# Two-block transformer on one core: gather, bias product and first expert weights reordered, neighbourhood scores computed two steps ahead, modulation groups regrouped

## The chip, the cores and the metric

The kernel runs on one core of one Trainium2 chip. The metric is the device time of one execution in microseconds (us), as the median of the runs. Engines by their names in the profile: PE is TensorE, DVE VectorE, ACT ScalarE, POOL GpSimd, SP SyncE, which here only starts transfers.

## What is computed

A batch of one with 256 tokens of width 1024 passes two blocks, all in fp32. The first block has a modulated mixer, a router that sends each token to 4 of 32 experts, and the experts. The second has two layers with modulated feed-forwards (SwiGLU, inner width 2816). Its layer 0 mixes by neighbourhood attention, which also looks at 256 context tokens, beside a multi-scale pool; its layer 1 by a short convolution. Cut to what the change touches:

```python
def moe_ffn(h, router_w, router_b, w1, b1, w2, b2):
    ...
    logits = (xt @ router_w + router_b).astype(jnp.float32)
    top_v, top_e = lax.top_k(logits, TOP_K)
    gate = jax.nn.softmax(top_v, axis=-1)
    ...
        hb = xb @ w1[e] + b1[e]
        ...
        return ((u + 1.0) * glu) @ w2[e] + b2[e]

def second_block(...):
    for i in range(DEPTH_2):
        m_l = adaln(c[:, None, :], mod_w[i], mod_b[i])         # 9 groups of 1024
        m_c = adaln(c_ctx[None, None, :], mod_w[i], mod_b[i])
        x = ffn_sublayer(x, m_l, norm_g[i, 0], ffn_w13[i, 0], ffn_w2[i, 0], 0)
        if ctx_here:
            ctx = ffn_sublayer(ctx, m_c, norm_g[i, 0], ffn_w13[i, 0], ffn_w2[i, 0], 0)
        xn = modulate(rms_norm_2(x, norm_g[i, 1]), m_l[:, :, 3], m_l[:, :, 4])
        if even:
            cn = modulate(rms_norm_2(ctx, norm_g[i, 1]), m_c[:, :, 3], m_c[:, :, 4])
            y_l, y_c = even_mixer(xn, cn, even_w_in[e], even_w_out[e], na_rpb[e], pool_w[e], pool_scale[e], ctx_out)
        ...
        x = x + m_l[:, :, 5] * y_l
        x = ffn_sublayer(x, m_l, norm_g[i, 2], ffn_w13[i, 1], ffn_w2[i, 1], 6)

def even_mixer(hl, hc, w_in, w_out, rpb, pool_w, pool_scale, ctx_out):
    q, k, v, u = jnp.split(hl @ w_in, [NA_WIDTH, 2 * NA_WIDTH, 3 * NA_WIDTH], axis=-1)
    k_c, v_c = jnp.split(hc @ w_in[:, NA_WIDTH:3 * NA_WIDTH], 2, axis=-1)
    att = neighbourhood_attention(split_heads(q), split_heads(k), split_heads(v), k_c, v_c, rpb)
    pool = multiscale_pool(u, pool_w, pool_scale)
    y_lat = jnp.concatenate([att, pool], axis=-1) @ w_out
```

## The kernel before

**Weights and ring.** All weights pass once through a ring in the on-chip memory. SP starts one transfer of 1 MB for each slot (128 partitions x 2048 numbers); in the experts and behind them the ring has eight places, and a transfer starts when the slot that held its place is released. The order of the slots in the stream is made ahead of the run by `make_plan` (class `Plan`), which also numbers the uses of PSUM.

**Products in parts.** From the experts on, an fp32 product is made of rounded parts: ScalarE copies a slot into one of four `w_high` buffers (L911 in the experts, L1005 later), VectorE subtracts that from the slot in place and gets `w_low` (L2228, L2364), and TensorE multiplies high by high, high by low and low by high (`split_gemm`, L1190; in the experts `w_high` and `w_low` by the gathered tokens `xg`, L1554). The activations' parts are `h_high` (ScalarE, `split_h`, L1018) and `h_low` (VectorE, `low_part`, L1871). Some products take fp32 straight from the ring, in one part (`gemm`, L1144).

**PSUM.** It is used in four places of two banks each, in strict rotation: use number u ("unit") takes place u mod 4, signals `psum_full` when TensorE has written it, and `psum_free` of its place when ScalarE or VectorE has read it.

**Order.** Nothing is scheduled by a tool. Each engine runs its own hand-written sequence, and semaphores keep the sequences together. So a step stands on its engine where the code calls it.

**Router to experts.** VectorE takes the four largest logits (L2144, L2146), fills unused entries of `vals` and `top` with very negative numbers (L2151, L2152, sixteen one-column memsets), marks the chosen experts (L2155, L2156) and builds the selection matrices `sel` (L2201) with their weights (L2206). ScalarE makes the exponentials (L888) and copies the turned gates (L893). TensorE turns the gates (L1503), multiplies them by `exp_b2` for the sum of output biases (L1511, units `bias_sum`; the transfer of `exp_b2` was issued by ScalarE at L872), and gathers the tokens of the first two experts by a product with `sel` (L1527, units `gather`). VectorE copies the bias sums into the accumulator (L2217); ScalarE copies the gathered tokens into `xg` (L897), then makes the first four `w_high` (L911). The experts run in 16 turns of two.

**Modulation.** Each group g of nine has four slots of weights. VectorE multiplies a slot by the condition and adds up in a buffer of `mod_sums` (`mod_slot`: L1815 for the first part, L1817 for the rest), TensorE sums the buffer over the partitions (`mod_sum`, L1269), VectorE finishes. There are three buffers (`MOD_SUMS`) in rotation; a group for two conditions (tokens and context: g 0 to 4 of layer 0) takes two of them and twice the VectorE work, one for one condition (5 to 8) takes one. The table `MODS` gives the order of the groups, and their slots are spread among the slots of the products.

**Layer 0 of the second block.** After the first feed-forward (on the tokens and the context together; L2404 multiplies the two halves of its hidden layer and so frees PSUM), `even_qk` and `even_vu` project the tokens and `even_ctx` the context. The normalised context is scaled by VectorE (L2433) and split by `split_h(6)` and `low_part(6)` into `h_high` and `h_low`, the buffers that the tokens' parts were in. The neighbourhood attention has eight steps (`NA_STEPS`: 2 blocks of queries x 4 pairs of heads). Of step s TensorE makes the scores (`na_scores`, L1688), VectorE adds the bias and takes the maximum (`na_soft`), ScalarE makes the exponentials `na_probs` (`na_exps`, L1096), TensorE turns them (L1736), ScalarE copies the turned ones (`na_turned`, L1103), TensorE multiplies them by the values (L1745), and VectorE scales the result (L2468). Scores of step s + 1 come ahead of the turn of step s. The pool's two products are L1714 and L1723, ahead of the first step. After the eighth step TensorE turns the outputs (L1753), ScalarE copies them into `cat` (L1116), and the output product `even_out` (L1144) runs over the eight chunks of `cat`, four of attention, then four of the pool. These lines are the whole of a step on TensorE and on ScalarE:

```python
            for s in range(len(NA_STEPS)):
                if s + 1 < len(NA_STEPS):
                    na_scores(s + 1)
                ...   # turn of s, L1736; wait for ACT's copy; output of s, L1745

            for s in range(len(NA_STEPS)):
                na_turned(s)
                if s + 1 < len(NA_STEPS):
                    na_exps(s + 1)
```

## Time and profile before

| | us |
|---|---|
| runs | 2950.53, 2966.67, 2951.52 |
| median | 2951.52 |
| the profiled execution | 2966.83 |
| its span on the core | 2964.8 |

| engine | busy us | share of the span | instructions |
|---|---|---|---|
| PE (products) | 2795.8 | 94% | 17548 |
| PEld (weight loads) | 2508.9 | 85% | 17548 |
| DVE | 2111.5 | 71% | 1868 |
| ACT | 1534.0 | 52% | 1294 |
| POOL | 9.7 | 0% | 7 |

The profiled execution moved 776 MB at 262 GB/s. The mean granted clock of TensorE was 0.954 of full speed. Times in rows count from the start of the span. PE stands for TensorE's products and PEld for its loading of the stationary operand, which runs beside them. A row of the timeline joins the instructions of one line that follow each other on an engine; "x" counts them (a plain fp32 product counts as two). "PEclk" is the granted clock, 1.00 for 2.4 GHz and 0.50 for 1.2 GHz. "[5.66 <-DVE w_low L2228]" says that the engine was idle for 5.66 us before, and that line 2228 of VectorE ended it. The stages that the change touches: router to experts at 446 to 492 us, experts 492 to 1577, first feed-forward of the second block about 1600 to 1920, projections and context projection to 2143, neighbourhood attention to 2212, its output product to 2242.

### The profile page before, as it was taken

The numbers are of one execution on the slowest core, as the hardware profiler recorded it, in microseconds if no ns is written. First come the engines' busy times: TensorE is split into PE (matmuls) and PEld (weight loads), VectorE is DVE, ScalarE is ACT, GpSimd is POOL, SyncE is SP. The second block draws the span as 40 slices with busy tenths as digits, with TensorE's granted clock in tenths as the row PEclk, the third lists the DMA queues.
The fourth block names the chain that finished last, engine by engine and source line by source line (L and its number), as shares of the span: only waits on it lengthen the run. The fifth ranks groups of instructions, "written<-read, shape, count | busy, mean of one in ns | idle before, by whom it ended". The sixth has DMA issues, their size and how long they took to land.

```text
span 2964.8 us, 43519 instructions
## 1 busy us (share of the span) xinstructions
PE 2795.8 (94%) x17548; PEld 2508.9 (85%) x17548; DVE 2111.5 (71%) x1868; ACT 1534.0 (52%) x1294; POOL 9.7 (0%) x7
## 2 busy tenths in 40 slices
PE   5999997999999999999997899999889999999998
PEld 5988886877877777777776899999869999999998
DVE  5335346999999999999998887676334766755454
ACT  0013315888888888888885334443333434433342
POOL 0000000000000000000000100000000000000000
PEclk8979897999999999999998899999979999999999
DMA  9753216999989999999996667777404776755462
GB/s 376 235 185 128 86 72 250 375 379 378 378 360 375 364 374 378 380 379 378 375 380 231 208 237 256 266 280 245 157 5 167 277 267 232 280 184 182 143 199 72
DMA packets 172401, 776.09 MB, mean 262 GB/s; under 512 B 12112, under 2 KB 37712, under 8 KB 121328
## 3 DMA queue, kind: packets, MB, share of 16 engines
q1 hardware_dynamic: 168352, 767.08, 68.8%
q10 hardware_dynamic: 3920, 7.11, 0.8%
q8 instruction: 102, 1.67, 0.2%
q14 instruction: 27, 0.22, 0.0%
HBM read 773.10 MB, written 1.05 MB: 261 GB/s over the span
## 4 chain that ended last, share of the span: by engine, by line
PE 65%; DVE 18%; issue 12%; ACT 4%; DMA 1%; DVEq 0%; ACTq 0%; SPq 0%
PE psum L1190 36%; DVE w_low L2228 10%; PE psum L1144 7%; PE psum L1554 5%; PE psum L1330 4%; PE psum L1591 2%; ACT w_high L911 2%; PE psum L1269 2%; PE psum L1527 1%; DVE mod_sums L1817 1%; DVE arena L2247 1%; PE psum L1288 1%; PE psum L1392 1%; PE psum L1344 1%; PE psum L1418 1%
## 5 line engine op out<-in xcount | busy, mean ns | idle before, releaser
L2228 DVE TENSOR_TENSOR w_low<-ring,w_high 128x2048 fp32r<-128x2048 f32 x396 | 882.0, 2285 | 40.6 <-ACT w_high L911 36.7
L911 ACT ACTIVATE w_high<-ring 128x2048 fp32r<-128x2048 f32 x396 | 736.7, 1907 | 95.7 <-PE psum L1554 94.0
L1005 ACT ACTIVATE w_high<-ring 128x2048 fp32r<-128x2048 f32 (+1 forms) x199 | 362.4, 1829 | 572.0 <-PE psum L1190 489.3
L2364 DVE TENSOR_TENSOR w_low<-ring,w_high 128x2048 fp32r<-128x2048 f32 (+1 forms) x199 | 432.4, 2183 | 307.3 <-ACT w_high L1005 304.7
L1190 PE MATMUL psum<-h_high,w_high 128*128 128x256 f32 x2144 | 610.8, 285 | 35.4 <-ACT h_high L1018 21.9
L1190 PE MATMUL psum<-h_low,w_high 128*128 128x256 f32 x2144 | 609.8, 286 | 7.8 <-DVE h_low L1871 7.8
L1190 PE MATMUL psum<-h_high,w_low 128*128 128x256 f32 x2144 | 611.9, 286 | 0.0
L1190 PEld LDWEIGHTS psum<-h_high,w_high 128*128 128x128 f32 x2144 | 415.8, 194 | 38.3 <-issue 24.0
L1190 PEld LDWEIGHTS psum<-h_low,w_high 128*128 128x128 f32 x2144 | 411.8, 193 | 8.1 <-DVE h_low L1871 8.0
L1190 PEld LDWEIGHTS psum<-h_high,w_low 128*128 128x128 f32 x2144 | 411.3, 192 | 0.0
L1554 PE MATMUL psum<-w_high,xg 128*128 128x512 f32 x1056 | 347.6, 410 | 16.7 <-DVE w_low L2228 11.7
L1554 PE MATMUL psum<-w_low,xg 128*128 128x512 f32 x1056 | 333.1, 397 | 0.0
L1817 DVE SCALAR_TENSOR_TENSOR mod_sums<-ring,cs,mod_sums 128x1024 f32<-128x1024 f32 x203 | 266.2, 1326 | 4.8 <-DMA ring<-in_mod_w 0.4
L1554 PEld LDWEIGHTS psum<-w_high,xg 128*128 128x128 f32 x1056 | 190.1, 189 | 89.9 <-DVE w_low L2228 48.6
L1190 PE MATMUL psum<-m_high,w_high 128*128 128x256 f32 x880 | 248.8, 283 | 0.0
L1190 PE MATMUL psum<-m_low,w_high 128*128 128x256 f32 x880 | 248.3, 282 | 0.0
L1190 PE MATMUL psum<-m_high,w_low 128*128 128x256 f32 x880 | 248.2, 282 | 0.0
L1554 PEld LDWEIGHTS psum<-w_low,xg 128*128 128x128 f32 x1056 | 199.2, 189 | 48.4
L1554 PE MATMUL psum<-w_high,hid 128*128 128x512 f32 x528 | 181.1, 425 | 26.7 <-DVE w_low L2228 20.0
L1554 PE MATMUL psum<-w_low,hid 128*128 128x512 f32 x528 | 170.7, 405 | 0.0
L1190 PEld LDWEIGHTS psum<-m_high,w_high 128*128 128x128 f32 x880 | 167.1, 190 | 0.1
L1190 PEld LDWEIGHTS psum<-m_low,w_high 128*128 128x128 f32 x880 | 166.9, 190 | 0.1
(267 smaller groups left out, 3258.8 us busy)
## 6 DMA issues: line engine op xcount, KB each, us to landing
ring<-in_exp_w SPq DMA_DIRECT2D x396, 1024.0 KB, 7.7
ring<-in_ffn_w SPq DMA_DIRECT2D x135, 1024.0 KB, 5.3
ring<-in_mod_w SPq DMA_DIRECT2D x96, 1024.0 KB, 5.5
ring<-in_ffn_w SPq DMA_DIRECT2D x40, 768.0 KB, 4.7
ring<-in_w_in SPq DMA_DIRECT2D x24, 1024.0 KB, 8.5
ring<-in_even_w_in SPq DMA_DIRECT2D x12, 1024.0 KB, 7.1
ring<-in_conv_w_in SPq DMA_DIRECT2D x12, 1024.0 KB, 5.0
ring<-in_w_branch SPq DMA_DIRECT2D x6, 1024.0 KB, 4.9
```

Of the source, the lines that this page charges most:

```text
L911: act.activation(high_ap(j, D), slot_ap(PLAN.moe_slot + j), ACT.Copy).then_inc(sem("expert_high_ready" + c.x), 1)
L1005: act.activation(high_ap(m, cols), slot_ap(s, 2, cols), ACT.Copy).then_inc(sem("w_high_ready"), 1)
L1144: mm = pe.matmul(unit(u0 + j // 4)[:, (j % 4) * T:(j % 4 + 1) * T], w[:, k % 2, (c0 + j) * P:(c0 + j + 1) * P], rhs(k), start=(k == 0 and ...
L1190: return pe.matmul(unit(u0 + j // 4)[:, (j % 4) * T:(j % 4 + 1) * T], w[:, k % 2, j * P:(j + 1) * P], h[:, k, :], start=first, stop=stop, ...
L1269: mm = pe.matmul(unit(u)[:, at:at + 1], mod_sums[:, MOD_BUFFERS[n][c], j * P:(j + 1) * P], ones[:, 0:1], start=True, stop=True)
L1288: mm = pe.matmul(unit(u)[:, 0:T], ones, squares[:, k, :], start=(k == 0), stop=(k == DC - 1))
L1330: mm = pe.matmul(unit(u)[:, j * T:(j + 1) * T], w[:, k, j * P:(j + 1) * P], hT[:, k, :], start=(k == 0 and j == 0), stop=(k == DC - 1), sk ...
L1554: mm = pe.matmul(u[:, cols], x_parts(k), w[:, k % 2, cols], start=(k == 0 and w is wh), stop=(k == DC - 1 and w is wl), skip_group_check=True)
L1591: mm = pe.matmul(c.unit(name)[:, (k % 4) * T:(k % 4 + 1) * T], moe_buf(f"y_rows{e}")[:, k * P:(k + 1) * P], moe_buf(f"selT{e}"), start=(e ...
L1817: last = dve.scalar_tensor_tensor(part, w[:, k % 2, :], cond, part, ALU.mult, ALU.add)
L2228: dve.tensor_tensor(low_ap(PLAN.moe_slot + j, D), slot_ap(PLAN.moe_slot + j), high_ap(j, D).bitcast(F32), ALU.subtract).then_inc(sem("expe ...
L2364: dve.tensor_tensor(low_ap(s, cols), slot_ap(s, 2, cols), high_ap(m, cols).bitcast(F32), ALU.subtract).then_inc(sem("w_split"), 1)
```

## The change

It edits seven things; nothing that is computed changes.

1. VectorE's memsets of `vals` are made before the mixer's output product; after the logits one `tensor_copy` of 2x4 columns takes the place of all sixteen.
2. TensorE gathers before it multiplies the biases. The units change places: `gather` had numbers 106 and 107 (places 2 and 3) and has 104 and 105 (places 0 and 1).
3. ScalarE makes `w_high` of slot 0 before the exponentials and of slots 1 to 3 before it copies the gathered tokens. VectorE copies the bias sums after the first four `w_low`.
4. The groups of the modulation for layer 0 come in the order 0, 1, 2, 5, 6, 3, 7, 4, 8 (before: 0 to 8).
5. The context's parts have buffers of their own, `ctx_high` and `ctx_low`, in free parts of the arena. Their making no longer waits for the last unit of `even_vu`, and `even_ctx` is called with `halves_last=True` and no `high_ready`.
6. `na_scores` of steps 0 and 1 come before the pool's first product; in step s the scores of s + 2 stand between the turn and the output of s. `na_probs` has two buffers. The pool's second product comes after step 0.
7. `even_out` takes its weights and the chunks of `cat` from the fifth on (pool first), and the turn of the outputs stands after its first two chunks of input.

```diff
-MODS = [(1, 0, g, 1) for g in range(6)] + [(2, layer, g, 2 if (layer, g) < (0, 5) else 1)
-                                           for layer in range(2) for g in range(N_MOD)]
+MODS = [(1, 0, g, 1) for g in range(6)] + \
+       [(2, layer, g, 2 if (layer, g) < (0, 5) else 1)
+        for layer in range(2) for g in ((0, 1, 2, 5, 6, 3, 7, 4, 8) if layer == 0 else range(N_MOD))]
...
-            self.stream.append((tensor, index, k, 2, col0, cols))
+            self.stream.append((tensor, index, (k + first) % k_chunks, 2, col0, cols))
...
-    p.unit("bias_sum", 2)
     p.pads = []
-    while p.n_units % 4 != 2:
+    while p.n_units % 4 != 0:
         p.pads.append(f"pad{len(p.pads)}")
         p.unit(p.pads[-1])
     p.unit("gather", 2)
+    p.unit("bias_sum", 2)
...
             p.unit("na_scores0")
             p.unit("na_vturn", 2)
+            p.unit("na_scores1")
             p.unit("pool_map")
-            p.unit("pool_out")
             for s in range(len(NA_STEPS)):
-                if s + 1 < len(NA_STEPS):
-                    p.unit(f"na_scores{s + 1}")
                 p.unit(f"na_turn{s}")
+                if s + 2 < len(NA_STEPS):
+                    p.unit(f"na_scores{s + 2}")
                 p.unit(f"na_out{s}")
+                if s == 0:
+                    p.unit("pool_out")
             p.unit("na_oturn")
-            p.gemm("even_out", "even_w_out", 0, DC, 0, D, 2)
+            p.gemm("even_out", "even_w_out", 0, DC, 0, D, 2, first=4)
...
-        na_probs = area(0, 2, 512)
+        na_probs = area(0, 2, 512), area(14336, 2, 512)
...
+        ctx_high = sb_at("ctx_high", [P, DC, T], F32R, arena_at)
+        ctx_low = sb_at("ctx_low", [P, DC, T], F32R, arena_at + 4 * 10240)
...
+            for q in PLAN.high_before:
+                await_release(act, q)
+
+            def high(c, *slots):
+
+                for j in slots:
+                    c.await_used(act, j - HIGHS)
+                    c.await_slot(act, j)
+                    act.activation(high_ap(j, D), slot_ap(PLAN.moe_slot + j), ACT.Copy).then_inc(
+                        sem("expert_high_ready" + c.x), 1)
+
+            high(first_turn(0), 0)
...
+            high(first_turn(0), 1, 2, 3)
...
-            high(first_turn(0), 0, 1, 2, 3)
+            for half in range(2):
+                await_unit(act, U["gather"] + half)
+                gathered(half, unit(U["gather"] + half), "")
...
-            high_parts(ahead_of("even_vu", HIGHS - 1))
-            await_unit(act, U["even_vu"] + 1)
-            split_h(6, ctx_scaled)
+            split_h(6, ctx_scaled, ctx_high)
...
-                if s >= 1:
-                    await_unit(act, U[f"na_turn{s - 1}"])
+                if s >= 2:
+                    await_unit(act, U[f"na_turn{s - 2}"])
...
             na_exps(0)
+            na_exps(1)
...
-            split_gemm("even_ctx", DC, DC, h_high, h_low, after_norm(6), high_ready=first_high(6))
+            split_gemm("even_ctx", DC, DC, ctx_high, ctx_low, after_norm(6), halves_last=True)
...
+            na_scores(1)
...
+                if s + 2 < len(NA_STEPS):
+                    na_scores(s + 2)
...
+                if s == 0:
+                    pooled()
+
+            def na_turned_in(k):
+                if k == 0:
+                    await_freed(pe, U["pool_out"])
+                if k == 2:
+                    await_freed(pe, U[f"na_out{len(NA_STEPS) - 1}"])
+                    u = U["na_oturn"]
+                    open_unit(pe, u)
+                    for c in range(4):
+                        for b in range(TB):
+                            mm = pe.transpose(unit(u)[:, c * T + b * P:c * T + (b + 1) * P],
+                                              na_o[:, b, c * P:(c + 1) * P], ident)
+                    mm.then_inc(psum_full, 1)
+                if k == 4:
+                    await_freed(pe, U["na_oturn"])
+
+            gemm("even_out", DC, DC, [(lambda k: cat[:, (k + 4) % DC, :], 0, DC)], na_turned_in, halves_last=True)
             for e in (2, 3):
                 norm(5 + e, hT)
                 ffn(e, 5 + e)
...
+            for n in range(4):
+                for b in range(TB):
+                    at = 36 * b + N_EXPERTS + n
+                    last = dve.memset(small[:, at:at + 1], -(n + 1.0) * 1e37)
+            link(last)
...
-            for n in range(4):
-                for b in range(TB):
-                    link(dve.memset(vals[:, 36 * b + E + n:36 * b + E + n + 1], -(n + 1.0) * 1e37))
-                    link(dve.memset(top[:, 8 * b + 4 + n:8 * b + 5 + n], -(n + 1.0) * 1e37))
+            link(dve.tensor_copy(top.rearrange("p (b e) -> p b e", b=TB)[:, :, 4:8],
+                                 vals.rearrange("p (b e) -> p b e", b=TB)[:, :, E:E + 4]))
...
             low(first_turn(0), 0, 1, 2, 3)
+            for half in range(2):
+                u = U["bias_sum"] + half
+                await_unit(dve, u)
+                free(dve.tensor_copy(acc[:, 4 * half:4 * half + 4, :], chunks(u)), u)
+                await_freed(dve, u)
...
+            for part in range(H_PARTS):
+                low_part(6, part, ctx_scaled, mod2[:, 0, 3, :, 1], ctx_low, ctx_high)
             low_parts(ahead_of("even_vu"))
-            for part in range(H_PARTS):
-                low_part(6, part, ctx_scaled, mod2[:, 0, 3, :, 1])
```

What stands in a row on the engines, before and now. Router to experts on ScalarE, from the copy of the turned hidden state (`h_nat_high`) to the expert loop (the `small` row is the exponentials, `arena` the turned gates, `xg` the gathered tokens). Before:

```order
L884 ACTIVATE h_nat_high<-psum 128x1024 x2
L888 ACT_TABLE_LOAD
L888 ACTIVATE small<-small 128x32 x2
L893 ACTIVATE arena<-psum 32x256
L897 ACTIVATE xg<-psum 128x1024 x2
L911 ACTIVATE w_high<-ring 128x2048 x4
```

After:

```order
L890 ACTIVATE h_nat_high<-psum 128x1024 x2
L899 ACTIVATE w_high<-ring 128x2048
L906 ACT_TABLE_LOAD
L906 ACTIVATE small<-small 128x32 x2
L911 ACTIVATE arena<-psum 32x256
L899 ACTIVATE w_high<-ring 128x2048 x3
L917 ACTIVATE xg<-psum 128x1024 x2
```

One of the four `w_high` copies now stands before the exponentials and three before the copies of the gathered tokens; the load of the table of functions comes after the first of them.

The same place on TensorE, which waits for `exp_b2`: the turn of the gates (`consts,small`), the bias product (`psum<-arena`) and the first three of the gather's 16 rows. Before:

```order
L1503 MATMUL psum<-consts,small 32x128 x2
L1511 MATMUL psum<-arena 128x256 x8
L1527 MATMUL psum<-sel,h_nat_high 128x2x64 x2
L1527 MATMUL psum<-sel,h_nat_low 128x2x64 x2
L1527 MATMUL psum<-sel,h_nat_high 128x2x64 x2
```

After, the last four of the gather's 16 rows, then the bias product:

```order
L1523 MATMUL psum<-sel,h_nat_high 128x2x64 x2
L1523 MATMUL psum<-sel,h_nat_low 128x2x64 x2
L1523 MATMUL psum<-sel,h_nat_high 128x2x64 x2
L1523 MATMUL psum<-sel,h_nat_low 128x2x64 x2
L1541 MATMUL psum<-arena 128x256 x8
```

The bias product has moved from before the sixteen rows of the gather to behind them.

VectorE in the first feed-forward, where it passes from modulation group 3 to 4 before, and from 5 to 6 now (`mod_sums` rows are modulation slots, `w_low` the weights of the product, the last row the product of the hidden halves that frees PSUM). Before:

```order
L2364 TENSOR_TENSOR w_low<-ring,w_high 128x2048
L1817 SCALAR_TENSOR_TENSOR mod_sums<-ring,cs,mod_sums 128x1024 x4
L2364 TENSOR_TENSOR w_low<-ring,w_high 128x2048 x2
L1817 SCALAR_TENSOR_TENSOR mod_sums<-ring,cs,mod_sums 128x1024 x4
L2364 TENSOR_TENSOR w_low<-ring,w_high 128x2048 x2
L1815 TENSOR_SCALAR mod_sums<-ring,cs 128x1024 x2
L1817 SCALAR_TENSOR_TENSOR mod_sums<-ring,cs,mod_sums 128x1024 x2
L2364 TENSOR_TENSOR w_low<-ring,w_high 128x2048 x2
L2404 TENSOR_TENSOR arena<-psum,arena 128x1024 x2
```

After:

```order
L2386 TENSOR_TENSOR w_low<-ring,w_high 128x2048
L1836 SCALAR_TENSOR_TENSOR mod_sums<-ring,cs,mod_sums 128x1024 x2
L2386 TENSOR_TENSOR w_low<-ring,w_high 128x2048 x2
L1836 SCALAR_TENSOR_TENSOR mod_sums<-ring,cs,mod_sums 128x1024 x2
L2386 TENSOR_TENSOR w_low<-ring,w_high 128x2048 x2
L1834 TENSOR_SCALAR mod_sums<-ring,cs 128x1024
L1836 SCALAR_TENSOR_TENSOR mod_sums<-ring,cs,mod_sums 128x1024
L2386 TENSOR_TENSOR w_low<-ring,w_high 128x2048 x2
L2426 TENSOR_TENSOR arena<-psum,arena 128x1024 x2
```

In the same places of the stream the slots have two or one partial sums where they had four or two.

ScalarE at the context's split (`rstd` row: the root of the norm; `arena<-psum` rows: results of `even_vu`). Before:

```order
L772 ACTIVATE arena<-arena 128x2048
L774 ACTIVATE rstd<-rstd 128x256
L1005 ACTIVATE w_high<-ring 128x2048 x3
L1018 ACTIVATE h_high<-arena,mod 128x256 x8
L1072 ACTIVATE arena<-psum 128x4x256
L1072 ACTIVATE arena<-psum 128x1024
L1005 ACTIVATE w_high<-ring 128x2048
```

After:

```order
L778 ACTIVATE arena<-arena 128x2048
L780 ACTIVATE rstd<-rstd 128x256
L1026 ACTIVATE ctx_high<-arena,mod 128x256 x8
L1013 ACTIVATE w_high<-ring 128x2048 x3
L1080 ACTIVATE arena<-psum 128x4x256
L1080 ACTIVATE arena<-psum 128x1024
L1013 ACTIVATE w_high<-ring 128x2048
```

The split of the context, into `ctx_high`, stands before the three `w_high` copies for `even_vu` instead of after them.

TensorE in the neighbourhood attention, from the scores of step 0 to the first step (128x512: scores; `consts`: turns, those with x16 of the values, those with x8 of a step; `vecs`: the pool's first product; 128x256: its second; 128x64: output). Before:

```order
L1688 MATMUL psum<-arena 128x512 x2
L1704 MATMUL psum<-consts,arena 128x128 x16
L1714 MATMUL psum<-vecs,arena 128x128 x8
L1723 MATMUL psum<-arena 128x256 x8
L1688 MATMUL psum<-arena 128x512 x2
L1736 MATMUL psum<-consts,arena 128x128 x8
L1745 MATMUL psum<-arena 128x64 x8
```

After:

```order
L1696 MATMUL psum<-arena 128x512 x2
L1712 MATMUL psum<-consts,arena 128x128 x16
L1696 MATMUL psum<-arena 128x512 x2
L1723 MATMUL psum<-vecs,arena 128x128 x8
L1745 MATMUL psum<-consts,arena 128x128 x8
L1696 MATMUL psum<-arena 128x512 x2
L1756 MATMUL psum<-arena 128x64 x8
L1734 MATMUL psum<-arena 128x256 x8
L1745 MATMUL psum<-consts,arena 128x128 x8
```

Scores of step 1 have moved before the pool's first product, scores of step 2 between the turn and the output of step 0, and the pool's second product behind that output.

## Rows read from the trace of the kernel before

**Rows 1.** Busy time by stretch; columns: stretch, us, PE PEld DVE ACT POOL, PEclk, DMA share, GB/s.
```profile
446.00:492.00 46.00, 28.88 (x130) 25.21 (x128) 21.61 (x74) 16.72 (x23) 0.00 (x0) 0.63 0.53 209
492.00:1577.00 1085.00, 1054.46 (x5216) 853.30 (x5216) 1044.08 (x748) 903.03 (x613) 0.00 (x0) 0.99 0.93 373
1860.00:2091.00 231.00, 231.00 (x1929) 230.20 (x1928) 155.46 (x121) 96.34 (x72) 0.00 (x0) 1.00 0.75 266
```

**Rows 2.** Timeline, router to experts; columns: start us, us, work, [idle before <-releaser].
```profile
462.91 0.06 DVE L2151 MEMSET small<- 128x1 f32 x1
...
464.81 0.06 DVE L2152 MEMSET small<- 128x1 f32 x1
...
469.35 0.90 DVE L2206 TENSOR_TENSOR arena<-sel,small 128x128 f32<-128x128 f32 x4
...
487.16 7.30 ACT L911 ACTIVATE w_high<-ring 128x2048 fp32r<-128x2048 f32 x4
...
491.86 1.22 PE L1554 MATMUL psum<-w_high,xg 128*128 128x512 f32 x2 [5.66 <-DVE w_low L2228]
...
495.64 59.13 SPq L670 DMA_DIRECT2D ring<-in_exp_w  x23
```

**Rows 3.** Chain of waits from 446 us; columns: start us, us, engine and line.
```profile
472.02 7.16 PE psum L1511 x16
479.18 7.03 PE psum L1527 x32
```

**Rows 4.** DMA issues, 440 to 480 us; columns: work, KB each, median us to landing.
```profile
arena<-in_exp_b ACTq DMA_DIRECT2D x1, 128.0 KB, 21.0
```

**Rows 5.** Busy time in four microseconds of the gather.
```profile
480.00:484.00 4.00, 4.00 (x21) 4.00 (x21) 0.52 (x1) 1.02 (x1) 0.00 (x0) 0.50 0.00 0
```

**Rows 6.** First feed-forward: waits (total us, times, longest us), timeline, busy time.
```profile
DVE mod_sums L1815 <- PE psum L1269: 23.6, 2, 13.1
...
1747.97 0.58 PE L1190 MATMUL psum<-h_high,w_high 128*128 128x256 f32 x1 [5.38 <-DVE arena L2404]
...
1748.00:1752.00 4.00, 4.00 (x20) 4.00 (x21) 3.96 (x4) 2.07 (x2) 0.00 (x0) 0.56 0.00 0
```

**Rows 7.** Chain of waits, one modulation sum for one condition.
```profile
1859.17 1.68 PE psum L1269 x16
```

**Rows 8.** Context projection: a chain row with its steady rate, then timeline.
```profile
1802.39 56.79 PE psum L1190 x480
...
2094.08 3.26 DVE L2433 SCALAR_TENSOR_TENSOR arena<-arena,mod,rstd 128x256 f32<-128x256 f32 x8
...
2108.32 0.28 PE L1190 MATMUL psum<-h_high,w_low 128*128 128x256 f32 x1
...
2118.33 1.01 PE L1190 MATMUL psum<-h_low,w_high 128*128 128x256 f32 x3 [7.85 <-DVE h_low L1871]
...
2142.67 0.28 PE L1190 MATMUL psum<-h_high,w_low 128*128 128x256 f32 x1
```

**Rows 9.** Timeline of TensorE in the neighbourhood attention.
```profile
2156.22 1.13 PE L1688 MATMUL psum<-arena 64*128 64x512 f32 x4
2157.28 1.09 PE L1736 MATMUL psum<-consts,arena 128*128 128x128 f32 x8
...
2161.59 2.08 PE L1688 MATMUL psum<-arena 64*128 64x512 f32 x4
...
2166.26 2.14 PE L1745 MATMUL psum<-arena 128*128 128x64 f32 x16 [1.11 <-ACT arena L1103]
2168.32 2.08 PE L1688 MATMUL psum<-arena 64*128 64x512 f32 x4
...
2204.93 3.67 PE L1745 MATMUL psum<-arena 128*128 128x64 f32 x16 [1.11 <-ACT arena L1103]
2209.05 1.97 PE L1753 MATMUL psum<-consts,arena 128*128 128x128 f32 x8 [0.46 <-DVE arena L2468]
2212.14 29.67 PE L1144 MATMUL psum<-arena,ring 128*128 128x256 f32 x128 [1.11 <-ACT arena L1116]
```

110 lines of the change are left out of this document (43 added, 67 removed).

## The prediction

> **What bounds the kernel now.** I read the busy time by stage first [rows 1]. From 492 to 1577 us run the experts: TensorE 1054 of 1085 us, VectorE 1044, the DMA engines 0.93 of the time. Nothing in the change alters this loop, so a gain must come from the places where TensorE stands still outside it. Between 446 and 492 us TensorE is busy for 28.9 of 46 us at 0.63 of its clock. Then I followed the chain of waits and the timeline through four places where TensorE waits: router to experts [rows 2 to 5], the first feed-forward [rows 6], the context projection [rows 8], the neighbourhood attention [rows 9]. Since TensorE is what ends last nearly everywhere else, a wait taken from it there is a gain of the whole.
>
> **Router to experts.** Today, in order: VectorE issues sixteen one-column memsets from 462.91 to 464.87, makes the selection, and its last part (470.25) lets the gather run [rows 2]. But TensorE has the bias product first. That starts at 472.02, runs 7.16 us, and the gather follows with 7.03 us to 486.2 [rows 3]. What the bias product waits for is `exp_b2`: issued at about 451, it took 21.0 us to land [rows 4]. After the gather ScalarE only starts the four `w_high` copies (487.16), and TensorE starts on the first weights at 491.86, after 5.66 us idle for `w_low` [rows 2].
> Now: the memsets shrink to one copy of 2x4 columns, about 0.1 us, so everything behind them comes 1.9 us sooner, the selection at 468.35. The gather runs 468.4 to 475.4 and the bias product, its input landed at 472, from 475.4 to 482.6. The weights are split by then: ScalarE makes `w_high` 0 before the exponentials, in time in which it waits today, and 1 to 3 before it takes the gather's result (4 x 1.83 us in all, done near 473.5); VectorE's four `w_low` (4 x 2.2) start after the busiest-expert steps at about 471.6 and end at 480.4; its two bias copies come after them. So the first expert product starts at 482.7 instead of 491.86: 9.1 us. I take off 0.8 for the clock: TensorE is at 0.50 there [rows 5], the first slot took 491.86 to 495.64, 3.8 us, and one slot more at 1.2 GHz would cost 1.9. **8.3 us.** The low end is 5.3 (that whole 1.9, and another 1.9 if the early `w_high` copy pushed the exponentials out by its full length); the high end is 9.1. The ring is full and the DMA queue stands until TensorE releases the first slot, at 495.64 [rows 2], so the weight stream moves forward with the start.
>
> **First feed-forward, modulation regrouped.** A group for two conditions needs two of the three sum buffers, so two such groups in a row collide: VectorE stood 23.6 us in two waits for TensorE's mod sums [rows 6]. The first wait costs TensorE nothing. After the second VectorE comes late with the weights and then with the product that frees PSUM, and TensorE idles 5.38 us until 1747.97; behind that it runs at 0.56 of the clock for 4 us [rows 6], some 16 products at 0.21 instead of 0.118 us, 1.5 us more. With one-condition groups 5 and 6 in these places the buffers don't collide and VectorE has half the work in each slot. 5.4 + 1.5 = **6.9 us**, between 4 (if part of VectorE's lateness stays) and 7.5. TensorE's own mod sums only change places: 32 products at two places fewer and at two more, where a one-condition sum took 1.68 us [rows 7]. VectorE's additional 2.4 us for each of eight slots fall in the output product of the first feed-forward and in the second one; in the 231 us from 1860 VectorE was busy for 155 and TensorE never waited [rows 1]. I count that at nothing; without this cover it would be up to the whole 19 us.
>
> **Context projection.** The context's high part shared `h_high` with the tokens, so ScalarE had to wait for the last product of `even_vu`, though VectorE had the scaled input from 2094.08 on. TensorE idles 7.85 us for the low part, with products at half speed behind it [rows 8]. The product takes from 2108.60 to 2142.95, 34.35 us, for 192 steps; the steady rate is 56.79 / 480 = 0.118 us, which makes 22.7 [rows 8]. With buffers of their own the parts are made by 2100.6 (3.3 us of scaling, the high parts beside it, 3.3 us of low parts) and the first two `w_low` by 2105.1, 3.5 us before they are wanted. 34.35 - 22.7 = 11.65, less 0.2 for small joints: **11.4 us**, from 10 to 11.65. The three high copies for the weights that ScalarE now starts after the split have the same 3.5 us of cover.
>
> **Neighbourhood attention.** Today a step is scores (S), turn (T), a wait for ScalarE's copy of the turned weights, output (O): 2161.59 to 2168.32, 6.73 us [rows 9]. The change puts the scores of two steps ahead between T and O, so that they cover the copy. But S, T and O themselves depend on the clock: 1.13, 1.09 and about 2.1 us at 2.4 GHz, 2.08, 1.97 and 3.67 at 1.2 GHz [rows 9] (1.97 is the last turn, with the same eight transposes). So a step without a wait takes 4.3 at the one level and 7.7 at the other. Today the clock swings between both within a step. As much time at either level would give 2 / (1/4.3 + 1/7.7) = 5.5; the O part, which the clock stretches most, and short waits for the exponentials make me take 5.7. Seven distances: 7 x 1.03 = 7.2 us. At the end the output product starts on its pool half at once instead of waiting 0.46 us for the last multiplication and 1.11 us for the copy, +1.6; at the start the pool product's first half moves behind the wait for the exponentials while S moves before it, -0.3. **8.5 us**, with ends of -5.4 and 17.
>
> **The sum** is 8.3 + 6.9 + 11.4 + 8.5 = 35.1 us. The profiled execution took 2966.83 us (span 2964.8 and 2.0 around it) and would take 2931.7. It stands 15 us above the median of 2951.52, beside the slowest of the three runs; none of the waits above depends on what makes that difference, so the sum goes off the median too: **2916 us**, 1.2% less.
>
> **Rivals.**
> (1) The attention runs at 1.2 GHz throughout: O is thin work for the array. 7.7 against 6.73 us in seven steps costs 6.8 instead of gaining 7.2: 2951.5 - 21.1 = 2930. For it: the last O ran so all through, and the gather and bias products, 14 us without a gap, never left 0.50 [rows 3, 5]. Against it: S is dense and comes in every step. Chance 0.10.
> (2) With the wait gone the clock stays up: 4.4 us a step, 7 x 2.3 = 16 instead of 7.2, 2907. For it: T and S ran at full level after the pool product [rows 9]. Against it, the same 14 us at 0.50. Chance 0.08. The Trainium skill's page TensorE: Matmul & The Clock Gate (section "HAM oscillation — how this bites in real kernels") says that idle gaps throttle TensorE and that work without gaps keeps it warm; by that rule this rival would be the forecast. The trace agrees only in part: after idle time the clock falls, but gapless gather and bias products did not raise it.
> (3) The experts swallow their earlier start, because the weight stream bounds them (DMA 0.93, [rows 1]): 8.3 less, 2925. Against it stands the queue's start at the first release. Chance 0.05.
> (4) The regrouping moves the wait instead of removing it: a two-condition group meets a held buffer at its new place. 6.9 less, 2923. The new order alternates conditions, and TensorE's sum for the earlier group lies tens of us before. Chance 0.04.
> (5) Slower: the earlier start leaves the ring of eight slots in another phase, and each of the 16 turns waits once more for a transfer of 1 MB, 2.75 us at the 373 GB/s of [rows 1]: 44 us, net 2960. It decides the sign from 2.2 us a turn. For it: VectorE and the DMA have only a few us of slack in a turn of 67. Against: all engines start shifted alike. Chance 0.03.
>
> **How the numbers follow.** The forecast keeps 0.70, with 2906 to 2928 from its own bounds. The range of 8 in 10 takes in (1) to (4), and a median beside the slowest run only in part: 2903 to 2934. About 0.5%, 15 us, is what a measurement of this kernel can tell from no change. Below 2936.8 lie the forecast and (1) to (4), 0.97, less 0.04 for (1) and (3) meeting runs 15 us up: faster 0.93. Within 0.5% 0.05, slower 0.02, mostly (5).
>
> **What would show it.** First expert product 9 us sooner after the last router product, with no wait for `w_low`; no wait of VectorE for mod sums in the first feed-forward and no 5 us idle of TensorE on the product's freeing; the context projection in about 23 us; attention steps near 5.7 us with the granted clock still swinging. Wrong would be: turns of the experts longer than 67.1 us, steps of 6.7 or more, or new idle time of TensorE before `w_low` in the second feed-forward.

## The result

| | before | changed |
|---|---|---|
| runs (us) | 2950.53, 2966.67, 2951.52, 2951.03 | 2913.44, 2915.34, 2918.91, 2918.91 |
| median (us) | 2951.28 | 2917.12 |
| ratio, 95% interval | | 0.9862, 0.9834 to 0.9890 |
| profiled execution, span (us) | 2966.83, 2964.8 | 2913.44, 2911.7 |

The changed kernel takes 34.2 us less, 1.4%; the forecast was 2916 us. The two profiled executions lie further apart than that, 53.4 us. Where those other 19 us belong turned out to be the main question of the experiments. The 34.2 us depend on which runs of before happened: three of its four lie near 2951 us and one near 2967, while beside the experiments it had medians of 2962.7, 2965.7 and 2964.7 us on three chips.

Stages of the changed kernel, busy time by stretch (columns as in [rows 1], which hold the same stages of before):

```profile
446.00:482.00 36.00, 27.88 (x126) 24.52 (x124) 25.91 (x60) 19.18 (x24) 0.00 (x0) 0.65 0.68 266
482.00:1567.00 1085.00, 1054.32 (x5217) 852.72 (x5216) 1039.19 (x746) 900.67 (x611) 0.00 (x0) 0.99 0.93 372
1834.00:2038.00 204.00, 204.00 (x1684) 203.58 (x1683) 150.89 (x122) 80.98 (x64) 0.00 (x0) 0.98 0.72 255
```

The experts are the same as before, TensorE busy for 1054 of 1085 us. TensorE's work from the router to the experts (27.9 us against 28.9) fits into 36 instead of 46 us. In the third stretch, most of the second feed-forward and the projections of the tokens, it never waits, as before, but its clock is 0.98 instead of 1.00.

Timeline of the changed kernel from router to experts, to be read beside [rows 2, 3]:

```profile
459.18 1.91 ACT L899 ACTIVATE w_high<-ring 128x2048 fp32r<-128x2048 f32 x1
462.27 0.16 DVE L2173 COPY small<-small 128x8 f32<-128x8 f32 x1
468.07 0.66 PE L1523 MATMUL psum<-sel,h_nat_high 128*128 128x128 f32 x2 [1.22 <-DVE arena L2228]
471.09 8.90 DVE L2245 TENSOR_TENSOR w_low<-ring,w_high 128x2048 fp32r<-128x2048 f32 x4
475.06 7.19 PE L1541 MATMUL psum<-arena 32*128 32x256 f32 x16
482.19 1.22 PE L1562 MATMUL psum<-w_high,xg 128*128 128x512 f32 x2
```

It runs as forecast: gather at 468.07 (forecast 468.4), bias product at 475.06, `w_low` ready at 480.0, and the first expert product directly behind the bias product at 482.19 (forecast 482.7), with no wait for `w_low`.

The context projection and the attention, timeline of TensorE, to be read beside [rows 8, 9]:

```profile
2087.34 0.28 PE L1197 MATMUL psum<-ctx_high,w_high 128*128 128x256 f32 x1
...
2110.15 1.13 PE L1696 MATMUL psum<-arena 64*128 64x512 f32 x4
...
2117.32 2.02 PE L1723 MATMUL psum<-vecs,arena 128*128 128x128 f32 x16 [2.95 <-ACT arena L1102]
...
2130.70 1.04 PE L1745 MATMUL psum<-consts,arena 128*128 128x128 f32 x8
2131.67 1.13 PE L1696 MATMUL psum<-arena 64*128 64x512 f32 x4
2133.47 2.00 PE L1756 MATMUL psum<-arena 128*128 128x64 f32 x16 [0.67 <-ACT arena L1109]
2135.30 1.04 PE L1745 MATMUL psum<-consts,arena 128*128 128x128 f32 x8
...
2150.65 2.00 PE L1756 MATMUL psum<-arena 128*128 128x64 f32 x16 [1.72 <-ACT arena L1109]
...
2156.48 8.81 PE L1151 MATMUL psum<-arena,ring 128*128 128x256 f32 x32
```

The projection takes 22.8 us (2087.34 to 2110.15) without a wait; before it took 34.35. An attention step, turn to turn, takes 4.60 us here (2130.70 to 2135.30); steps of 4.60 and of 3.99 us alternate, and all their parts run at full clock. The forecast was 5.7 us with the clock swinging. Two waits remain that the forecast put too low or did not name: 2.95 us for the first exponentials, and 1.72 and 1.11 us in the last two steps, which have no scores left to put in between. Behind these last waits the clock fell after all: the first 32 products of the output product take 8.81 us, where 48 take 10.52 at full clock later on.

### The profile page after: what moved, and what is told of

It is laid out like the page before. It is cut to its first block and busy times, and to the rows that moved or that the text cites. A ratio compares the mean times of both kernels' runs of the same rounds, so it can differ in the third digit from the quotient of the medians.

```text
span 2911.7 us, 43510 instructions
## 1 busy us (share of the span) xinstructions
PE 2771.8 (95%) x17548; PEld 2492.4 (86%) x17548; DVE 2111.8 (73%) x1861; ACT 1534.0 (53%) x1294; POOL 9.7 (0%) x7
## 5 line engine op out<-in xcount | busy, mean ns | idle before, releaser
L2386 DVE TENSOR_TENSOR w_low<-ring,w_high 128x2048 fp32r<-128x2048 f32 (+1 forms) x199 | 441.4, 2229 | 323.9 <-ACT w_high L1013 321.0
L1197 PE MATMUL psum<-h_high,w_high 128*128 128x256 f32 x2080 | 592.5, 285 | 27.4 <-ACT h_high L1026 21.6
L1197 PE MATMUL psum<-h_high,w_low 128*128 128x256 f32 x2080 | 595.0, 286 | 0.0
L1197 PE MATMUL psum<-h_low,w_high 128*128 128x256 f32 x2080 | 593.3, 287 | 0.0
L1197 PEld LDWEIGHTS psum<-h_high,w_high 128*128 128x128 f32 x2080 | 404.6, 195 | 29.7 <-issue 28.8
L1197 PEld LDWEIGHTS psum<-h_low,w_high 128*128 128x128 f32 x2080 | 398.9, 193 | 0.0
L1197 PEld LDWEIGHTS psum<-h_high,w_low 128*128 128x128 f32 x2080 | 397.2, 191 | 0.0
L1836 DVE SCALAR_TENSOR_TENSOR mod_sums<-ring,cs,mod_sums 128x1024 f32<-128x1024 f32 x203 | 257.4, 1283 | 4.9 <-DMA ring<-in_mod_w 0.4
```

The source lines that it names most:

```text
L1197: return pe.matmul(unit(u0 + j // 4)[:, (j % 4) * T:(j % 4 + 1) * T], w[:, k % 2, j * P:(j + 1) * P], h[:, k, :], start=first, stop=stop, ...
L1836: last = dve.scalar_tensor_tensor(part, w[:, k % 2, :], cond, part, ALU.mult, ALU.add)
L2386: dve.tensor_tensor(low_ap(s, cols), slot_ap(s, 2, cols), high_ap(m, cols).bitcast(F32), ALU.subtract).then_inc(sem("w_split"), 1)
```

## The experiments

Each kernel was run 6 or 12 times beside runs of before on the same chip. These runs of before are 63 in all, on three chips; the four of the result and the twelve of the next section come on top. Stage lengths below are differences of start times of TensorE's rows in the profiles. In those of before the first feed-forward runs from 1629 to 1861 us, the second to 2059 and the three projections to 2143; the section on the time before put the end of the first one too late.

### The kernel before, a second time

> The kernel before, unchanged, for a second profile and the spread of its runs. Question: the two traces differ by 53 us in their spans, the medians by 34 us. Theory 1: the profiled execution of before (2966.8 us) had TensorE's clock swinging in the neighbourhood attention (0.74, step 6.73 us), and the usual execution near 2951 us has it at 1.00 there: a profile near 2951 shows attention steps near 4.3 + 1.1 = 5.4 us and about 15 us less between 2143 and 2242 us, and nothing else shorter by more than 2 us. Theory 2: the 15 us lie elsewhere (the experts, or spread over the stages), and the attention is again at 6.7 us a step. If this profile falls near 2966 us it tells only where that kind of execution has its time.

12 runs from 2947.12 to 2970.83 us, ratio 1.0004 (0.9980 to 1.0028). They lie in two groups, six up to 2955.84 and six from 2964.04 on. The 29 runs of before on this chip do the same: 14 up to 2958.92 (median 2953.7) and 15 from 2962.66 on (median 2966.9). The new profile (2952.84 us) is of the lower group, the first one (2966.83 us) of the upper. The attention in the new profile:

```profile
2176.80 1.13 PE L1688 MATMUL psum<-arena 64*128 64x512 f32 x4
2177.86 1.09 PE L1736 MATMUL psum<-consts,arena 128*128 128x128 f32 x8
2180.07 2.00 PE L1745 MATMUL psum<-arena 128*128 128x64 f32 x16 [1.11 <-ACT arena L1103]
2182.00 1.13 PE L1688 MATMUL psum<-arena 64*128 64x512 f32 x4
```

The wait of 1.11 us for ScalarE's copy is the same as in [rows 9], but scores and turn take 1.13 and 1.09 us in every step. In the first profile they take 2.08 and 1.5 to 1.8 from the second step on; its first step ran at full clock too. A step takes 5.20 us (2176.80 to 2182.00) instead of 6.73. Busy time of the loop, of this profile and of the first one (columns as in [rows 1]):

```profile
2157.00:2195.00 38.00, 29.09 (x207) 22.16 (x206) 17.92 (x39) 18.33 (x36) 0.00 (x0) 1.00 0.00 1
```

```profile
2163.60:2204.90 41.30, 33.53 (x174) 23.72 (x172) 14.77 (x31) 15.19 (x31) 0.00 (x0) 0.75 0.00 0
```

The granted clock is 1.00 in the one and 0.75 in the other. From the first scores to the end of the output product the profiles take 84.0 and 98.8 us, 14.7 us apart. The steps make about 9.5 us of that; the rest is the last output, the turn of the outputs and the beginning of the output product, which ran at half clock in the first profile only. Up to the attention and behind it the two agree within 2 us. So the old attention loop has two courses with the same instructions and the same waits, one at full clock and one in which the clock swings. Theory 1 holds. That the courses make the two groups of runs is borne out by the later profiles: of the six kernels and executions that keep the old loop, the two with full clock in it (this one and the kernel with the context's buffers alone) have times of the lower group of their kernel, the four with 0.75 or 0.76 (the first of before, and the kernels with the router's part, with the modulation's order, and without the attention's part) times of the upper.

### The attention's part alone, and the rest without it

First the kernel before with items 6 and 7 of the change, the main lines:

```diff
+            p.unit("na_scores1")
...
+                if s + 2 < len(NA_STEPS):
+                    na_scores(s + 2)
...
+        na_probs = area(0, 2, 512), area(14336, 2, 512)
...
+            gemm("even_out", DC, DC, [(lambda k: cat[:, (k + 4) % DC, :], 0, DC)], na_turned_in, halves_last=True)
```

> Before with the attention's part of the change alone (scores two ahead, second probabilities buffer, pool product after step 0, rotated output product). Theory 1 (most of the 22 us that the traces show here is the clock of one profiled execution): 2951 - 8 = 2943 us, between 2939 and 2946, steps near 4.3 us at clock 1.00. Theory 2 (all 22 us are the change's): 2929 us.

2948.52 us (12 runs, 2937.41 to 2952.34), ratio 0.9952 (0.9932 to 0.9971). That is 5.2 us below the lower group of before and 18.4 below the upper one. Theory 2 (2929 us) is out; theory 1 is near, but its range ended at 2946. The steps are 3.99 and 4.60 us at full clock, as in the changed kernel. But here the clock fell in the last two steps, behind the wait of 1.72 us:

```profile
2181.97 1.04 PE L1741 MATMUL psum<-consts,arena 128*128 128x128 f32 x8
2184.73 3.14 PE L1752 MATMUL psum<-arena 128*128 128x64 f32 x16 [1.72 <-ACT arena L1106]
2187.66 1.91 PE L1741 MATMUL psum<-consts,arena 128*128 128x128 f32 x8
2190.69 3.67 PE L1752 MATMUL psum<-arena 128*128 128x64 f32 x16 [1.11 <-ACT arena L1106]
```

The output parts take 3.14 and 3.67 us instead of 2.00, and the whole stage 82.3 us; in the changed kernel's two profiles it takes 76.6 and 78.1. The runs of this kernel spread over 15 us, in no two clear groups.

Then the changed kernel with items 6 and 7 undone, of which the main lines:

```diff
-                if s + 2 < len(NA_STEPS):
-                    na_scores(s + 2)
+                if s + 1 < len(NA_STEPS):
+                    na_scores(s + 1)
```

> The changed kernel with the attention's part undone. By the traces the other three parts give 9.5 + 10.6 + 11.6 = 31.7 us. Theory 1: 2951 - 29 = 2922 us (2918 to 2926), 5 above the changed kernel. Theory 2: 2917 + 22 = 2939 us, with the context projection still at 23 us.

2934.93 us (6 runs, 2922.72 to 2940.17), ratio 0.9907 (0.9875 to 0.9939). The profile (2939.04 us) took the swinging course, steps of 6.83 us and 97.4 us for the stage. The runs spread over 17 us, as a loop with two courses does; its two lowest runs stand 5 to 9 us above the changed kernel, its three highest 20 to 23, and one lies between them at 15. Neither theory's single number (2922 and 2939 us) describes that: both were written as if a kernel had one time.

### The modulation groups alone

```diff
-MODS = [(1, 0, g, 1) for g in range(6)] + [(2, layer, g, 2 if (layer, g) < (0, 5) else 1)
-                                           for layer in range(2) for g in range(N_MOD)]
+MODS = [(1, 0, g, 1) for g in range(6)] + \
+       [(2, layer, g, 2 if (layer, g) < (0, 5) else 1)
+        for layer in range(2) for g in ((0, 1, 2, 5, 6, 3, 7, 4, 8) if layer == 0 else range(N_MOD))]
```

> Before with the new order of the modulation groups alone. Forecast 6.9 us: 2944 us, TensorE's 5.38 us idle before the first product behind L2404 gone, VectorE's waits for mod sums gone. By the two traces the part gave 10.6 us: 2940.5 us. If only the first feed-forward gains and the second gives part back beyond TensorE's own mod sums, 2947 us.

2958.67 us (12 runs), ratio 0.9992 (0.9971 to 1.0012), far from the 2944 us expected: the median alone can't tell this part, because the attention takes one course or the other. Four runs lie near 2950 us and eight at 2956 and above; their medians, 2949.7 and 2961.9, stand 4 and 5 us below those of before's groups. The profile tells more. At the first scores it stands 6.7 us ahead of the second profile of before (2136.16 against 2142.82), where 6.9 were forecast: the first feed-forward, to the start of the second, takes 220.3 instead of 232.0 us, and the second one 203.4 instead of 198.7. The idle 5.38 us and VectorE's waits for mod sums are gone. Of the 11.7 us gained in the first, 4.7 come back in the second.

### The changed kernel, a second time

> The changed kernel, unchanged, for the spread of its runs and a second profile of the attention. In the second profile of before (2951 us) the attention ran at full clock with steps of 5.20 us, in the first (2966 us) it swung, 6.73 to 6.83 us; about half of before's runs lie in each group. Theory 1: the new loop leaves TensorE so little idle time that only the full-clock course is left, 12 runs lie within 10 us, steps are again 4.3 us, and the median is about 2917 us. Theory 2: the new loop has two courses as well, and some runs lie 10 to 15 us above the others (steps of 5.8 us or more).

2917.98 us (6 runs, 2916.02 to 2924.18), ratio 0.9861 (0.9830 to 0.9893), and steps of 3.99 and 4.60 us again. With the four runs of the result that makes ten runs within 11 us, where 63 runs of before show 29 and 34 in two groups with medians 13 to 15 us apart. Theory 1 holds as far as ten runs can show it; the kernels mask_late and split_sums below have the same loop, and their runs spread over 8.4 and 6.5 us. The profile has a difference to the first: the router's products, which make the logits, ran at half clock, 6.87 us instead of 4.04, and from the turn of the hidden state before them to the first expert product it took 3.1 us more:

```profile
456.60 6.87 PE L1491 MATMUL psum<-vecs,hT 128*128 128x32 f32 x32
```

### Router to experts alone, and the context's buffers alone

Items 1 to 3 of the change on the kernel before, the main lines:

```diff
+            high(first_turn(0), 0)
...
+            high(first_turn(0), 1, 2, 3)
...
             low(first_turn(0), 0, 1, 2, 3)
+            for half in range(2):
+                u = U["bias_sum"] + half
```

> Before with the part from the router to the experts alone. The traces give the first expert product 9.1 us earlier and the experts' end 9.9 us earlier: group by group of runs 9.5 us below before, 2942 us in the low group and 2957 in the high one. Rival: the experts' weight stream swallows the earlier start, no difference.

2952.93 us (12 runs), ratio 0.9970 (0.9945 to 0.9994). Group by group: 2943.5 and 2958.95 against 2951.5 and 2966.9 of before on this chip, 8 us in either, where 9.5 were expected. In its profile the router's products ran at half clock too, and from the turn of the hidden state to the first expert product it took 31.2 us; where this part is as before it was 37.1 to 37.4 in every profile, and it was 28.1 in the changed kernel's first. Experts took 1096.8 us from their first to their last `xg` product, before 1096.1 to 1096.9: nothing is swallowed.

Item 5 on the kernel before, the main lines:

```diff
-            high_parts(ahead_of("even_vu", HIGHS - 1))
-            await_unit(act, U["even_vu"] + 1)
-            split_h(6, ctx_scaled)
+            split_h(6, ctx_scaled, ctx_high)
```

> Before with the context's own buffers alone. Forecast 11.4 us: the context projection takes 23 instead of 34.4 us, the low group of runs at 2940 us, the high one at 2955. If the clock behind it falls because the order of loads changed, under 8 us.

2944.43 us (12 runs), ratio 0.9956 (0.9933 to 0.9979). Divided between 2945.91 and 2950.25, a gap less clear than in before, the groups have medians of 2941.2 and 2955.25, 10.3 and 11.7 us below those of before. From the start of the three projections (`even_qk`) to the first scores the profile takes 71.9 us, before 83.3 and 83.5: 11.4 us, the forecast to the tenth.

### Scores one step ahead

The changed kernel, with the order turn of s, scores of s + 1, output of s, the main lines:

```diff
-                if s + 2 < len(NA_STEPS):
-                    na_scores(s + 2)
+                if s + 1 < len(NA_STEPS):
+                    na_scores(s + 1)
```

> The changed kernel with the attention's scores one step ahead instead of two: in step s the order is turn of s, scores of s + 1, output of s. Theory 1 (the second step of distance is what hides the softmax): by the trace of the changed kernel a turn can start 4.75 us after the start of its scores, and the scores start 0.97 us after the turn before, so a step takes 5.7 us instead of 4.3, with a wait before each turn; 7 x 1.4 = 10 us more, 2928 us at full clock, and more if the clock falls in the waits. Theory 2 (it is enough that something stands between turn and output): 2918 us.

2937.03 us, six runs from 2936.63 to 2938.03, ratio 0.9925 (0.9899 to 0.9951). It is theory 1, with a higher price than its 2928 us, because the clock did not stay up. Timeline of TensorE:

```profile
2152.45 1.97 PE L1742 MATMUL psum<-consts,arena 128*128 128x128 f32 x8
2154.35 2.08 PE L1694 MATMUL psum<-arena 64*128 64x512 f32 x4
2156.36 3.67 PE L1753 MATMUL psum<-arena 128*128 128x64 f32 x16
2160.17 1.97 PE L1742 MATMUL psum<-consts,arena 128*128 128x128 f32 x8
```

This step is 7.72 us, all of it at 1.2 GHz with hardly a wait: the 7.7 us that the prediction gave its rival (1). The time until the exponentials are there fits into the parts stretched to double length. Of the other steps the first, at full clock, took the expected length (5.85 us); two more took 7.72 and two 7.3 and 7.5, and these have waits of 1.69 or 1.82 us or parts at full clock in them. The mean clock from 2137 to 2175 us was 0.63. So the three loops can be set side by side. With a wait of 1.7 to 1.8 us in a step the clock came down in the one profile, and the six times, within 1.4 us, make the same course likely for all runs. With 1.11 us in each step it stayed down in four of six profiles. With 0.67 us in every other step the steps between the first and the last two ran at full clock in all five profiles of that loop.

### GpSimd's masking moved behind the first feed-forward

The changed kernel, and on GpSimd one wait more, for the end of the first feed-forward:

```diff
             pool.wait_ge(sem("rpb_landed"), 16 * ROWS)
+            pool.wait_ge(sem("x_ready"), 3)
```

> The changed kernel with GpSimd's masking of the position bias (9.4 us, beside VectorE's first work of the first feed-forward) moved behind that feed-forward. In both traces VectorE's partial sums beside it take 3.5 instead of 1.3 us each, and TensorE then stands 5.2 us (6.5 before) for the low parts of the weights. Theory 1: the two share a port or the memory, the partial sums go back to 1.3 us, the wait goes, and the kernel takes 6 us less, 2911 us. Theory 2: the slowness belongs to the place and not to GpSimd: no change.

2912.03 us (6 runs), ratio 0.9836 (0.9805 to 0.9867), against 2917.98 of the changed kernel on the same chip. The place in the changed kernel, and the same work in this one:

```profile
1636.75 13.37 DVE L2386 TENSOR_TENSOR w_low<-ring,w_high 128x2048 fp32r<-128x2048 f32 x2
1638.66 9.31 POOL L745 TENSOR_TENSOR arena<-arena,consts 128x4096 f32<-128x4096 f32 x1 [1638.21 <-DMA arena<-in_rpb]
...
1650.27 0.55 PE L1197 MATMUL psum<-h_high,w_high 128*128 128x256 f32 x1 [5.16 <-DVE w_low L2386]
```

```profile
1637.38 4.50 DVE L2387 TENSOR_TENSOR w_low<-ring,w_high 128x2048 fp32r<-128x2048 f32 x2
...
1826.90 8.97 POOL L746 TENSOR_TENSOR arena<-arena,consts 128x4096 f32<-128x4096 f32 x1 [1826.45 <-DVEq L1813]
...
1829.37 8.90 DVE L1837 SCALAR_TENSOR_TENSOR mod_sums<-ring,cs,mod_sums 128x1024 f32<-128x1024 f32 x2
```

Two `w_low` take 13.37 us beside GpSimd and 4.50 without it. The excess, 8.87 us, is nearly GpSimd's whole 9.31. At 2.25 us each the first would end at 1639.00, GpSimd ends at 1647.97, and the second ends one length behind that, at 1650.12: one of the two stood still until GpSimd was done. The expectation's reading of before (partial sums of 3.5 us each) was an average over one held instruction and three normal ones. At its new place GpSimd holds up one of two partial sums (8.90 us for the two, 2.48 elsewhere), and TensorE does not wait behind it. The Trainium skill's page SBUF — State Buffer (section "SBUF: two separate sides") says that VectorE and GpSimd share a pair of ports under an exclusive lock, and that an instruction of VectorE with two inputs from this memory waits for one of GpSimd that reads it; by that rule the trace agrees. The 5.16 us of TensorE and the half clock behind them are gone: from the first feed-forward's start to the second's the profile takes 6.0 and 7.0 us less than the changed kernel's two.

### Sums for two conditions divided

On top of the kernel mask_late, the main lines:

```diff
+                    if MODS[n][3] == 2:
+                        mod_sum(n, (0,))
+                        late = n
...
+                                   high_ready=first_high(normed) if first else None, between=second_sum)
```

> The kernel mask_late with TensorE's modulation sums for two conditions divided: the sum for the tokens stays, the one for the context comes 48 products later, in the next product. In the traces a sum for two conditions (32 one-column products in a row, 3.6 us) is followed by about 4 us at 0.57 of the clock, one for one condition (16, 1.8 us) is not. Theory 1: the clock falls because of the length of that stretch; divided, three falls of some 1.7 us go, 2912 - 5 = 2907 us. Theory 2: any such sum may bring it down, or VectorE's later wait for the whole sum costs as much: no change, or up to 5 us slower.

2908.39 us (6 runs), ratio 0.9830 (0.9804 to 0.9856). The second condition's sum now comes 48 products later for two of the three such groups; the third lies behind an output product and stayed whole. Busy time just behind the group at 1895 us, of mask_late and of this kernel (columns as in [rows 1]):

```profile
1896.00:1900.00 4.00, 4.00 (x30) 4.00 (x30) 2.22 (x2) 2.22 (x2) 0.00 (x0) 0.79 0.94 324
1900.00:1904.00 4.00, 4.00 (x21) 4.00 (x20) 3.37 (x5) 0.00 (x0) 0.00 (x0) 0.50 0.66 269
1904.00:1908.00 4.00, 4.00 (x31) 4.00 (x31) 0.00 (x0) 0.02 (x1) 0.00 (x0) 0.86 0.00 0
```

```profile
1899.00:1903.00 4.00, 4.00 (x37) 4.00 (x35) 0.76 (x1) 0.64 (x1) 0.00 (x0) 1.00 0.69 282
1903.00:1907.00 4.00, 4.00 (x35) 4.00 (x36) 2.86 (x4) 1.27 (x1) 0.00 (x0) 1.00 0.82 264
1830.00:1834.00 4.00, 4.00 (x24) 4.00 (x23) 4.00 (x1) 0.00 (x0) 4.00 (x1) 0.57 1.01 412
```

TensorE is busy all the time in both (4.00 of 4.00 us). The clock falls behind the whole sum and doesn't behind the divided ones, and it does fall at 1830 in this kernel too, behind the sum that was left whole. The fall behind a whole sum is the rule, though not without exception: over all profiles it came behind 36 of 38. One of the two others is the first such sum of the kernel without the attention's part:

```profile
1682.00:1686.00 4.00, 4.00 (x37) 4.00 (x36) 0.90 (x3) 0.00 (x0) 0.00 (x0) 1.00 0.18 68
```

A sum for one condition (16 products) was never followed by a fall where TensorE went on without a wait. Where it stands ahead of the first feed-forward's output product, with a wait of 0.8 to 1.2 us behind it, the clock fell in eight of nine profiles. The second feed-forward takes 3.9 us less and the first 1.3. The medians stand 3.6 us apart, on different chips; that the part is worth 4 to 5 us is read from the traces, the runs don't show it by themselves.

### The attention's remaining waits filled, and all together

On top of the kernel mask_late, the units and with them the work in this order, and the output of the last step (`half_done`) behind the first eight products of `even_out` (in fp32, 16 in a row), the main lines:

```diff
+            p.unit("pool_map")
             p.unit("na_scores0")
+            p.unit("pool_out")
             p.unit("na_vturn", 2)
             p.unit("na_scores1")
...
+                    if half == 0 and half_done:
+                        half_done()
```

> The kernel mask_late with the attention's remaining waits filled: the pool's two products around the first scores (TensorE waits 2.95 us for the first exponentials there today), and the first eight products of the output product between the last turn and the last output (1.11 us). 2.5 + 1.1 = 3.6 us less, 2908.5 us, if the clock stays at 1.00 in the attention. Rival: the first steps now wait for ScalarE and VectorE instead (their copies and the pool's scaling come in a row), no gain.

2907.36 us (6 runs, 2902.88 to 2909.68), ratio 0.9826 (0.9800 to 0.9852). From the start of the two projections to the end of the output product the profile takes 143.1 us (73.7 and 69.5), mask_late 150.0 (71.9 and 78.1): 6.9 us, where 3.6 were expected. In mask_late the clock had fallen behind the wait of 2.95 us (the pool's first product took 3.56 us there, 2.02 at full clock) and again at the start of the output product; here it stays up in both places. The end of the attention and the output product:

```profile
2144.00:2175.00 31.00, 31.00 (x163) 27.70 (x163) 12.09 (x13) 11.14 (x9) 0.00 (x0) 1.00 0.20 68
```

The kernels mask_late, split_sums and fill in one:

> mask_late, split_sums and fill together: 2912 - 5 - 3.6 = 2903 us; if only one of the two holds, 2907 us.

2899.65 us (6 runs, 2894.75 to 2905.77), ratio 0.9793 (0.9767 to 0.9820): 65 us below before's median on that chip, 52 to 54 below the medians of before's lower groups, and 17.5 us below the changed kernel's median. This version beats both. (Its runs, like those of split_sums and fill, are from another chip than those of mask_late; the runs of before had the same two groups there, with medians of 2952.4 and 2966.3 us.)

## Why the prediction was right, and where it was not

**The total** was right, 2916 against 2917.1 us, and that was in part luck: the attention's term came out of two errors that cancelled, and the median that the sum was taken off was one in which the lower group of before had three of four runs. In 34 of 63 runs before is in the upper group. From a median of 2965.7, as on the chip of the changed kernel's second profile, the same sum gives 2930.6 us; the changed kernel has 2918.0 there. Against the second profile of before (2952.84 us, lower group) the changed kernel's two profiles give:

| part | forecast | measured |
|---|---|---|
| router to experts | 8.3 (5.3 to 9.1) | 9.3, or 6.2 with the router at half clock |
| modulation regrouped | 6.9 (4 to 7.5) | 8.8 to 11.1; alone 7.0 |
| context projection | 11.4 (10 to 11.65) | 11.4 |
| attention and output product | 8.5 (-5.4 to 17) | 5.9 to 7.4; against the first profile 20.7 to 22.2 |

The parts make 39.2 and 32.3 us; the two executions stand 39.4 and 35.7 below that of before, so up to 3.4 us lie outside the four places.

**Router to experts: right.** Each start came within about 0.5 us of the forecast. The 0.8 us taken off for the clock was not lost. That the router's own products sometimes run at half clock was not foreseen; it happened in three of the nine profiles that have this part and in none of the five without it, which is too few to lay it on the change.

**Modulation: right in sum, by other terms.** The 5.38 us and the half clock behind them went, and alone the new order gave 7.0 us. But that is 11.7 gained in the first feed-forward and 4.7 lost in the second. What the forecast did not see is a price of the sums for two conditions that no idle time shows: the clock falls behind them. Before had three in the first feed-forward, and the clock behind each:

```profile
1690.00:1694.00 4.00, 4.00 (x21) 4.00 (x21) 1.83 (x3) 0.12 (x1) 0.00 (x0) 0.51 0.50 202
1738.00:1742.00 4.00, 4.00 (x22) 4.00 (x23) 3.64 (x4) 0.00 (x0) 0.00 (x0) 0.59 0.23 95
1791.00:1795.00 4.00, 4.00 (x20) 4.00 (x20) 3.93 (x3) 3.69 (x4) 0.00 (x0) 0.50 0.32 130
```

Of these one now stands in the second feed-forward, and one at the very end of the first, so that its fall lands in the second. VectorE's additional work there was counted at nothing, and rightly: TensorE is busy for 204.00 of 204 us. But "TensorE's own mod sums only change places" was meant as free on balance, and in the second feed-forward it hides 16 products more (1.8 us) and two falls of the clock. In the changed kernel the first feed-forward gained more than alone, 15.2 to 16.3 us. That is not the order's doing: TensorE's two waits near GpSimd's masking took 5.8 us in its first profile instead of the 8.0 with the order alone, and some falls were shorter.

**Context projection: right**, 22.8 us for a forecast of 22.7 to 23.

**Attention: the wrong step.** It was this sentence: the sum goes off the median too, since none of the waits depends on what makes the 15 us between the profiled execution and the median. They were in the attention, in the very rows from which its term was worked out [rows 9]. Read rightly, those rows describe one of two courses; the change was worth 18 us there and 5 to 7 in the other, from which the median of 2951.5 came. The second error lay in the step itself: 5.7 us with the clock between its levels, where it is 4.3 at full clock. That was rival (2), with a chance of 0.08, and its step of 4.4 us was right. In seven distances from turn to turn the forecast took 7 x 6.73 = 47.1 us off and put 7 x 5.7 = 39.9 on. At full clock the old loop has 35.2 (the first profile has 44.7, since its first step was short and its last has no scores), and the new one 29.8 without the pool's product. So the two errors, 11.9 and 10.1 us, met in 7.2 for a measured 5.4. The +1.6 at the end came only to 0.3, since the clock fell at the start of the output product, and the -0.3 at the start came to between +0.2 and +1.7. The rivals (1), (3), (4) and (5) did not come; (1) came, in part, in the kernel with scores one step ahead.

Of the rule of the Trainium skill weighed there (page TensorE: Matmul & The Clock Gate, section "HAM oscillation — how this bites in real kernels"), the runs show this: fewer gaps did keep the clock up, as it says, but the same gap of 1.11 us in each step left the clock at 1.00 in some executions and at 0.75 in others, and gapless one-column sums brought it down.

## What to carry to other kernels

A profile is one execution: where it stands away from the median, find the stage that makes the difference (a second profile and stage lengths do it in one run) before taking any stage's price from it. In a loop on TensorE with a short wait in each step, count a wait's price at both clock levels; taking the wait down far enough may be worth less than it seems in a slow profile and still remove most of the spread. The latter held for the changed kernel and what was built on it (6 to 11 us), not for the attention's part alone (15 us). Look behind long stretches of very thin products too: the clock can fall there with no idle time to show it, and dividing the stretch is cheap.

## What was not expected of the hardware

- One program has two courses of TensorE's clock. With the same instructions and the same wait of 1.11 us in each step, the steps took 5.20 us each at clock 1.00 in one execution, and in another, from the second on, about 6.73 us each at 0.75; 29 and 34 of 63 runs of before lie in the two groups. What tips an execution into one or the other stays open: the two profiles agree within 2 us all the way up to the attention. No experiment tried to steer it.
- A stretch of 32 one-column products, 3.6 us long and without a gap, was followed in before by 4 us at 0.50 to 0.59 of the clock, and over all profiles by a fall in 36 of 38 cases. Behind 16 of them (1.8 us) with no wait after them there was none, and behind 32 divided by 48 full products there was none in four cases.
- One instruction of VectorE stood still for nearly the whole 9.3 us of one instruction of GpSimd (13.37 us for two that take 4.50).
